# Down projections of three feed-forward blocks: 512-column products in three of four column groups, and banks emptied in two parts

## What is computed

```python
x = x + mix
x = x + _conv_ffn(_rmsnorm(x, norm_ffn[i]), ...)       # (silu(gate) * up) @ w_down
x = _rmsnorm(x, norm_final)
...
x = x + 0.5 * (1 + ga1[:, None, :]) * swiglu(h, w1_gate[l], w1_up[l], w1_down[l])
...
x = x + 0.5 * (1 + ga3[:, None, :]) * swiglu(h, w2_gate[l], w2_up[l], w2_down[l])
```

## Time and profile before

| | |
|---|---|
| median of 3 runs | 807.7 us (807.48 to 807.9) |
| the profiled execution's own time | 807.91 us |
| its span, first to last instruction | 806.1 us |
| PE busy | 790.8 us (98%), 6800 products |
| DVE busy | 647.3 us (80%) |
| ACT busy | 482.1 us (60%) |
| mean DMA | 223 GB/s |

### The profile page before, as it was taken

One profiled execution on the slowest core, in us unless ns is written; L12 is line 12 of the kernel. 1 busy time (PEld: TensorE's weight loads), 2 busy tenths in 40 slices (PEclk: granted clock), 3 DMA queues, 4 the chain that ended last, 5 costly groups with the idle time before them and its releaser, 6 DMA issues.

```text
span 806.1 us, 16841 instructions
## 1 busy us (share of the span) xinstructions
PE 790.8 (98%) x6800; PEld 774.1 (96%) x6800; DVE 647.3 (80%) x1389; ACT 482.1 (60%) x1002; POOL 25.1 (3%) x57
## 2 busy tenths in 40 slices
PE   8999999999999999999999999899999999999998
PEld 7999999999999999999999999878889999999998
DVE  5888888998889897999988887977767996675551
ACT  6755567667766666745554645665666765555440
POOL 1000000000000000000000002700000000000000
PEclk9999999999999999999999999999999999999999
DMA  9776784655666987599989887555334678655640
GB/s 293 266 257 225 221 288 156 210 187 185 204 222 201 324 283 257 176 320 352 345 307 317 291 257 236 162 158 153 110 112 150 190 257 260 219 180 191 197 157 27
DMA packets 150014, 179.45 MB, mean 223 GB/s; under 512 B 5680, under 2 KB 139568, under 8 KB 149936
## 3 DMA queue, kind: packets, MB, share of 16 engines
q1 hardware_dynamic: 147680, 177.22, 66.8%
q10 hardware_dynamic: 1232, 1.11, 0.4%
q0 software_dynamic: 1024, 0.03, 0.1%
HBM read 177.27 MB, written 1.05 MB: 221 GB/s over the span
## 4 chain that ended last, share of the span: by engine, by line
PE 84%; DVE 10%; ACT 3%; issue 1%; DMA 1%; SPq 0%; DVEq 0%
PE bank L1460 25%; PE bank L1463 25%; PE bank L1464 25%; DVE wlo L1036 3%; PE bank L1449 2%; PE bank L1574 1%; PE bank L1451 1%; PE bank L1450 1%; DMA raw<-in_moba_w_qkv 1%; PE bank L1519 1%; DVE mring L1135 1%; PE bank L1536 1%; DVE W L1362 0%; ACT whi L794 0%; DVE yb L1086 0%
## 5 line engine op out<-in xcount | busy, mean ns | idle before, releaser
L1036 DVE TENSOR_TENSOR wlo<-raw,whi 128x512 fp32r<-128x512 f32 x528 | 342.4, 683 | 60.3 <-ACT whi L794 59.8
L794 ACT ACTIVATE whi<-raw 128x512 fp32r<-128x512 f32 x528 | 306.4, 622 | 96.7 <-PE bank L1464 85.5
L1460 PE MATMUL bank<-A,whi 128*128 128x256 f32 x1152 | 322.9, 280 | 2.2 <-DVE wlo L1036 1.3
L1463 PE MATMUL bank<-A,whi 128*128 128x256 f32 x1152 | 318.8, 277 | 0.1
L1464 PE MATMUL bank<-A,wlo 128*128 128x256 f32 x1152 | 318.5, 276 | 0.0
L1460 PEld LDWEIGHTS bank<-A,whi 128*128 128x128 f32 x1152 | 216.3, 188 | 4.3 <-DVE wlo L1036 2.4
L1463 PEld LDWEIGHTS bank<-A,whi 128*128 128x128 f32 x1152 | 216.4, 188 | 0.7 <-issue 0.5
L1464 PEld LDWEIGHTS bank<-A,wlo 128*128 128x128 f32 x1152 | 216.4, 188 | 0.0
L1460 PE MATMUL bank<-Hhi,whi 128*128 128x256 f32 x528 | 146.0, 276 | 0.0
L1464 PE MATMUL bank<-Hhi,wlo 128*128 128x256 f32 x528 | 145.7, 276 | 0.0
L1463 PE MATMUL bank<-Hlo,whi 128*128 128x256 f32 x528 | 145.7, 276 | 0.0
(11 more groups left out here) (172 smaller groups left out, 960.0 us busy)
## 6 DMA issues: line engine op xcount, KB each, us to landing
mring<-in_w_mod SPq DMA_DIRECT2D x72, 512.0 KB, 6.7
raw<-in_ffn_w_up SPq DMA_DIRECT2D x22, 1024.0 KB, 5.1
raw<-in_w_gate SPq DMA_DIRECT2D x22, 1024.0 KB, 6.0
raw<-in_w_up SPq DMA_DIRECT2D x22, 1024.0 KB, 5.6
raw<-in_w_down SPq DMA_DIRECT2D x16, 1024.0 KB, 5.5
raw<-in_w_in SPq DMA_DIRECT2D x12, 1024.0 KB, 5.7
raw<-in_moba_w_qkv SPq DMA_DIRECT2D x11, 1024.0 KB, 5.4
raw<-in_ffn_w_down SPq DMA_DIRECT2D x8, 1024.0 KB, 6.1
```

The lines of the kernel that those rows point to most:

```text
L794: act.activation(whi[:, i % SPL, k0:k1, 0:width], raw[:, i % RAW, k0:k1, 0:width], ACT.Copy).then_inc(s_whi, 1)
L1036: dve.tensor_tensor(lo, raw[:, i % RAW, k0:k1, 0:width], hi.bitcast(F32), ALU.subtract).then_inc(s_wlo, 1)
L1460: pe.matmul(o, hi, xh, start=kg == 0 and not (j and halved(g)), stop=False)
L1463: pe.matmul(o, hi, xl, start=False, stop=False)
```

## The change

The hidden activations become one tensor `H` with high and low part of a tile side by side, 512 columns. In the first three column groups of each of the three down phases (`wide`), the two products with the weight's high part become one product with these 512 columns. Its output fills the whole bank: columns 0 to 255 hold high by high, columns 256 to 511 high weight by low activation. The product with the weight's low part is as before and adds to columns 0 to 255. When such a group is emptied, DVE adds columns 256 to 511 to `XT` first, waits for that (new semaphore `s_xlow`), and then adds columns 0 to 255 as before. The fourth group of each down phase and all other phases are as they were.

```diff
--- before.py
+++ after.py
@@ -523,8 +523,8 @@
         rcol = sb("rcol", [P, 8])
         sb("pad_h", [P, PAD_H])
         with ExitStack() as scope:
-            Hhi = scope.enter_context(nc.sbuf_tensor("Hhi", [P, KF, S], F32R))
-            Hlo = scope.enter_context(nc.sbuf_tensor("Hlo", [P, KF, S], F32R))
+            H = scope.enter_context(nc.sbuf_tensor("H", [P, KF, 2, S], F32R))
+        Hhi, Hlo = H[:, :, 0, :], H[:, :, 1, :]
         Ohi = sb("Ohi", [P, KD, S], F32R)
         Olo = sb("Olo", [P, KD, S], F32R)
         Vn = sb("Vn", [P, 2, D])
@@ -562,7 +562,7 @@
         s_scores, s_max, s_exp, s_inv, s_scale = (sem(n) for n in ("s_scores", "s_max", "s_exp", "s_inv", "s_scale"))
         s_stick, s_sp, s_lb = sem("s_stick"), sem("s_sp"), sem("s_lb")
         s_tpe, s_tfree, s_w, s_val, s_ohi, s_olo = (sem(n) for n in ("s_tpe", "s_tfree", "s_w", "s_val", "s_ohi", "s_olo"))
-        s_lsum, s_vn, s_rcol = sem("s_lsum"), sem("s_vn"), sem("s_rcol")
+        s_xlow, s_lsum, s_vn, s_rcol = sem("s_xlow"), sem("s_lsum"), sem("s_vn"), sem("s_rcol")
         s_gq, s_qsq, s_qln, s_qr, s_qkn = (sem(n) for n in ("s_gq", "s_qsq", "s_qln", "s_qr", "s_qkn"))
         s_f1, s_f2, s_f3, s_f4, s_flo, s_fsplit, s_fset = (sem(n) for n in ("s_f1", "s_f2", "s_f3", "s_f4", "s_flo", "s_fsplit", "s_fset"))
 
@@ -614,6 +614,10 @@
             if halved(g):
                 return banks[2 * (g % 2)][:, i * S + c0:i * S + c1]
             return banks[2 * (g % 2) + i][:, c0:c1]
+
+        def wide(g):
+
+            return groups[g][1] == "down" and groups[g][2] < 3 * C
 
         def pair_of(g):
 
@@ -1025,6 +1029,7 @@
         @block.vector
         def _(dve):
             need = Once(dve)
+            lows = [0]
             dve.memset(epsc[:, 0:1], EPS).then_inc(s_eps, 1)
             dve.memset(epsc[:, 1:2], EPS * EPS).then_inc(s_eps, 1)
             dve.memset(shb[:, :, :], 0.0).then_inc(s_shb0, 1)
@@ -1275,6 +1280,15 @@
                             need.wait_ge(s_latey, 8 * LATE_OF["up4"] + n + 1)
                             need.wait_ge(s_alo, 32 + n + 1)
                             need.wait_ge(s_acc, acc_index["up4", 3, 0])
+                        if wide(g):
+                            b2 = at(g, i, S, 2 * S)
+                            if not gate:
+                                dve.tensor_tensor(x, b2, x, ALU.add).then_inc(s_xlow, 1)
+                            else:
+                                dve.scalar_tensor_tensor(out=x, in0=b2, scalar=hcol[:, n:n + 1], in1=x,
+                                                         op0=ALU.mult, op1=ALU.add).then_inc(s_xlow, 1)
+                            lows[0] += 1
+                            need.wait_ge(s_xlow, lows[0])
                         if not gate:
                             ins = dve.tensor_tensor(x, b, x, ALU.add)
                         else:
@@ -1449,6 +1463,14 @@
                         pe.matmul(o, xh[:, q], hi, start=kg == 0 and not j, stop=False)
                         pe.matmul(o, xl[:, q], hi, start=False, stop=False)
                         ins = pe.matmul(o, xh[:, q], lo, start=False, stop=final and j == 1)
+                    if kt % 2 == 1:
+                        ins.then_inc(s_chunk, 1)
+                    return
+                if wide(g):
+                    for j in range(2):
+                        hi, lo = whi[:, i % SPL, kt, j * P:j * P + P], wlo[:, i % SPL, kt, j * P:j * P + P]
+                        pe.matmul(at(g, j, 0, 2 * S), hi, H[:, kg, :, :].rearrange("p a b -> p (a b)"), start=kg == 0, stop=False)
+                        ins = pe.matmul(at(g, j), lo, xh, start=False, stop=final)
                     if kt % 2 == 1:
                         ins.then_inc(s_chunk, 1)
                     return
```

## The result

The changed kernel takes 815.2 us (median of 4, 814.76 to 815.57) against 807.8 for the kernel before (median of 4, 807.48 to 808.07): ratio 1.0092, interval 1.0076 to 1.0108. It is 7.4 us slower; the prediction said 2.4 us faster. The profiled execution took 814.76 us with a span of 813.0, so 6.9 us more span than before.

The account below looks back on a forecast made before the run. The prediction took PE's product count times distance to bound the down phases. From the profiled 807.9 us, less 2.6 saved on PE plus 0.2 wait, gave 805.5, or 805.3 against the median; range 803.1 to 809.2.

Parts of the forecast that it names:

- The bound: Down phases: PE waits for nobody, so time is the number of products times their distance, taken as 113.3 ns.
- T(512): Forecast time of one 512-column product in the down phases: 220.0 ns, with ends 215.6 and 224.3.
- narrow groups that change their 276: Sign that the forecast is wrong: 256-column products in each down phase's unchanged last column group no longer 276 ns long.
- The saving of 2.6 us: PE in the down phases: 396 merged pairs with their third product, 333.3 ns instead of 340, 6.7 saved each.
- rival 3: Down phases: mixed lengths make every product pay 4.5 ns more, narrow groups too; 2.9 us lost, 810.6 us; chance 0.18.
- the 0.2 for a wait: After the first down phase: PE waits 0 to 0.5 us for activation tiles or norm sums; 0.2 us entered.
- Rival 1: Down products: the 4.3 ns beyond bf16's fixed part go with columns; 1.0 us saved, less 0.2; 806.9 us; chance 0.21.
- Rival 2: Down products: 256 columns just fail to cover the next weight load, 512 cover it; 4.4 us saved, 803.5; chance 0.17.
- The adds: VectorE emptying wide banks: four chained adds, about 1.75 us instead of 0.75; +1.0 us a group, mostly hidden.
- The backlog at the end of the first down phase: VectorE falls behind in groups two to four; the last group's x comes 2.0 us later relative to PE.
- Rival 4: VectorE, behind in the first down phase, costs 1 to 3 us instead of 0.2; 807.7 to 808.5 us; chance 0.06.
- Layout, DMA and the end: H's new strides, the same DMA bytes, and the 3.5 us after PE's last product: no effect on time.

## Why the prediction was wrong

**The bound.** Right. A down phase is the number of products times their distance, and PE waits for nobody there, before and after.

**The step that failed.** The forecast priced a pair at 220.0 + 113.3 ns and left the narrow groups at 276: it took the good rhythm to outlive the arrival of 512-column products. It doesn't. From the first wide product on a pair takes 353.3 ns and a narrow product 117.8, and six such products were enough for the whole loss. That is about 7.5 us of the 9.9 by which 815.2 exceeds the 805.3 of the forecast. Some 2 us more are a term of the sum that was mis-sized, T(512) in the good rhythm. The prediction's own sign of being wrong, narrow groups that change their 276, was met.

**T(512).** This term was too small. I took the 6.7 ns by which a product exceeds 2.4 columns a ns for a fixed part, since the float32 rows have a fixed part that stays with length. Those are products of another operand type. Here the excess goes with the columns: 225 to 226 ns was measured for a product of 512 in the good rhythm, not 220, which is just above my high end of 224.3. The saving of 2.6 us would have been 0.3 to 0.7. I had the row that spoke for it: 256 columns in bf16 have 109 and in this type 113.3, and the difference had no reason to be fixed. I chose by which rows *varied* the length, not by which were of the same kind.

**The pair in the slow rhythm.** Another failure, in the price of rival 3. Its mechanism, the loss of the good rhythm in wide and narrow groups, is what happened, and the narrow groups' +4.5 ns was sized right (1.8 us). But I added 4.5 ns once to the 512-column product, 224.5, on top of the same fixed part. Per column it is twice that on twice the base: 2 x 117.8 = 235.6, and 235.0 was measured. With it rival 3 would have read 353.4 a pair, 13.4 x 396 = 5.3 us, and with 1.8 and 0.2 a time of 815.0. The measured one is 815.2; the 0.2 for a wait is in that sum and was not there, so the agreement is that much luck. The forecast's sign is wrong because rival 3 was held for unlikely (0.18), and its upper end is too low because rival 3 was priced at 810.6.

**The chance of rival 3.** "Many such stretches end by themselves after a few products" was put against it. True for some, but in the down phases a slow stretch that outlived the first few products lasted to the end of the phase, over 500 products, unless a one-column product ended it. What the earlier trace rows shows, 87 products in an o group at 281 throughout, was the better hint.

**Rival 1** (columns set the time) had T(512) nearly right, and 806.9; it lacked the state, which made the sign. **Rival 2** (the load) falls for the wide products: under a product of 225 ns, which covers its load wholly (188 ns in the profile), the time per column is hardly better (0.439 against 0.443). It isn't settled for 256 columns, as a short product shows: 128 and 192 columns take 57 and 86 ns, but the product behind then takes 171 and 141, so that both together need 228 and 227, twice the ordinary distance. As if no product could have less than a slot of some 114 ns for its load. That is a guess: no run changed the load, and none tells whether this also holds the 256-column ones back. The Trainium skill ("TensorE: Matmul & The Clock Gate", section "LDWEIGHTS (loading the stationary operand)") gives a load 107 ns for 128 columns, as an estimate from that page: near it, but no run here shows that figure itself.

**The adds.** The cost of four adds, +1.0 us forecast, was +0.93. The backlog at the end of the first down phase, 2.0 us forecast, was 0.3 us, since the groups grew by 0.55 us instead of shrinking by 0.3: three groups gave it 3 x 0.85 = 2.5 us of room that the sum didn't have. The wait of PE was 0 (0.2 entered). **Rival 4** falls with it.

**Layout, DMA and the end** at nothing: right. The layout alone is 0.9995, and beyond the three phases the span changes by less than 0.1 us.

**What stays open:** what in the chip makes the two rhythms, which product starts the slow one, why an unmixed stream of 512 columns does not leave it behind, and why a one-column product ends it in the down phases but not always elsewhere.

## What to carry to other kernels

Before merging products to save their fixed part, measure that the type at hand has one: put one product of the new length into the running stream and read the distance behind it. And read the products behind it too: one product of another length can set the pace of the next 500. Where the same instruction shows two durations in a trace, price a change by both, in proportion to the product's columns, and ask what it would do to the places that it doesn't touch.

## What was unexpected of the hardware

- A stream of products of this operand type (256 columns, 128 x 128 weights) has two steady rhythms at the same granted clock (1.00, the upper level, 2.4 GHz): 113.3 and 117.8 ns. One product of 512, 320 or 128 columns, or a bf16 one of 256, was enough to move it from the first to the second, and it then held over more than 500 products. One of 192, 260, 288 or 384 columns was not. Each length but 512 was tried once.
- A one-column float32 product, 0.14 us, moved it back in the down phases: 815.6 and 809.7 us are the times of two kernels that differ in three such products.
- A product of 512 columns takes 225 to 226 ns in the good rhythm and 235.0 in the slow; an unmixed stream of them 233.3, alternating between 231 and 236, and the 256-column products behind that stream were in the good rhythm.
- Products of 128 and 192 columns take 57 and 86 ns in a stream of 256 columns, but the next one takes 171 and 141: 228 and 227 for both, twice the ordinary distance.
- 260 columns, alone in the stream, take 116 ns; in the groups in which all have 258 or 260, they are 120.3 to 120.4 apart, and 121.9 with 264.
